# Half of the columns in the recurrence levels of a three-layer kernel

## The reference, cut to what matters

```python
def rwkv7_scan(r, w, k, v, kk, a):
    decay = jnp.exp(-jnp.exp(w))
    b = kk * a
    def step(S, inp):
        r_t, d_t, k_t, v_t, kk_t, b_t = inp
        sa = jnp.einsum('bhij,bhj->bhi', S, -kk_t)
        S = S * d_t[:, :, None, :] + sa[..., None] * b_t[:, :, None, :] + v_t[..., None] * k_t[:, :, None, :]
        return S, jnp.einsum('bhij,bhj->bhi', S, r_t)
```

## Time and profile before

| | |
|---|---|
| median of 3 runs | 3526.99 us |
| time of the profiled execution | 3526.12 us |
| its span | 3524.0 us |
| TensorE busy | 3456.2 us (98% of the span) |
| VectorE, ScalarE, GpSimd busy | 2423.2, 1642.0, 289.4 us |
| mean granted TensorE clock | 0.995 |
| the six pairs of the recurrence | from about 371 to 692 us |

### The profile page before, as it was taken

The page is one execution under the profiler, slowest core; times in us unless marked ns, Lnnn a source line. Parts: engine busy times, 40 slices in busy tenths (PEclk is TensorE's granted clock), DMA queues, the critical chain, the costliest instruction groups (busy, mean ns, idle before and its releaser), DMA issues.

```text
span 3524.0 us, 75021 instructions
## 1 busy us (share of the span) xinstructions
PE 3456.2 (98%) x27870; PEld 3151.2 (89%) x27870; DVE 2423.2 (69%) x3490; ACT 1642.0 (47%) x2248; POOL 289.4 (8%) x358
## 2 busy tenths in 40 slices
PE   8999999999999999999999999999999999999998
PEld 8999888899988899999888888888899988888886
DVE  6986777755676677976756565677766865656566
ACT  6456334444444434754444444444444644434344
POOL 5000234200020000002000000020000200000002
PEclk9999999999999999999999999999999999999999
DMA  7444222255655555555565555555554555555564
GB/s 253 160 156 144 86 86 86 82 171 179 204 191 188 184 178 175 168 169 181 185 194 181 194 185 193 182 188 191 174 161 162 173 185 185 191 185 194 181 194 140
DMA packets 164985, 604.04 MB, mean 171 GB/s; under 512 B 18336, under 2 KB 18464, under 8 KB 164560
## 3 DMA queue, kind: packets, MB, share of 16 engines
q1 hardware_dynamic: 163584, 596.16, 51.8%
q10 hardware_dynamic: 1040, 3.16, 0.2%
q0 software_dynamic: 192, 2.23, 0.2%
HBM read 599.38 MB, written 2.10 MB: 171 GB/s over the span
## 4 chain that ended last, share of the span: by engine, by line
PE 90%; DVE 6%; ACT 2%; issue 1%; POOL 0%; DMA 0%; ACTq 0%; DVEq 0%; POOLq 0%
PE bank L366 35%; PE bank L369 18%; PE bank L345 11%; PE bank L346 10%; PE bank L347 10%; PE bank L1349 4%; DVE w_lo L334 2%; ACT w_hi L325 1%; POOL x_norm_acc L466 0%; DVE nrm_kk L1039 0%; DVE X L2900 0%; PE bank L848 0%; DVE X L2904 0%; PE bank L731 0%; DVE conv_sq L2584 0%
## 5 line engine op out<-in xcount | busy, mean ns | idle before, releaser
L325 ACT ACTIVATE w_hi<-raw 128x1024 fp32r<-128x1024 f32 x1126 | 1157.6, 1053 | 827.2 <-PE bank L369 510.5
L334 DVE TENSOR_TENSOR w_lo<-raw,w_hi 128x1024 fp32r<-128x1024 f32 x1126 | 1350.0, 1236 | 99.9 <-ACT w_hi L325 99.6
L366 PE MATMUL bank<-hid,w_hi 128*128 128x512 f32 x2048 | 643.4, 395 | 0.0
L366 PE MATMUL bank<-u,w_hi 128*128 128x512 f32 x1536 | 484.4, 397 | 0.0
L345 PE MATMUL bank<-hx,w_hi 128*128 128x256 f32 x1568 | 466.1, 297 | 12.1 <-DVE w_lo L334 12.1
L369 PEld LDWEIGHTS bank<-hid,w_lo 128*128 128x128 f32 x2048 | 384.7, 188 | 90.9
L346 PE MATMUL bank<-hx,w_hi 128*128 128x256 f32 x1568 | 445.3, 284 | 0.0
L347 PE MATMUL bank<-hx,w_lo 128*128 128x256 f32 x1568 | 444.9, 284 | 0.3 <-issue 0.3
L366 PE MATMUL bank<-xh,w_hi 128*128 128x512 f32 x1312 | 413.5, 397 | 2.7 <-DVE w_lo L334 2.7
L369 PE MATMUL bank<-hid,w_lo 128*128 128x256 f32 x2048 | 402.3, 278 | 0.0
L369 PEld LDWEIGHTS bank<-u,w_lo 128*128 128x128 f32 x1536 | 289.5, 189 | 69.2
(11 more groups left out here) (477 smaller groups left out, 5559.3 us busy)
## 6 DMA issues: line engine op xcount, KB each, us to landing
raw<-stream SPq DMA_DIRECT2D x1126, 512.0 KB, 4.0
x_raw<-xT SPq DMA_DIRECT2D x4, 512.0 KB, 7.5
mem_raw<-memT ACTq DMA_DIRECT2D x4, 512.0 KB, 9.5
x_res<-xT POOLq DMA_DIRECT2D x1, 2048.0 KB, 9.7
out<-X SPq DMA_DIRECT2D x3, 512.0 KB, 2.7
cst<-consts SPq DMA_DIRECT2D x1, 1504.0 KB, 13.6
out<-X SPq DMA_DIRECT2D x2, 256.0 KB, 2.2
w_sb<-w ACTq DMA_DIRECT2D x1, 384.0 KB, 4.8
```

Of the source, the lines that this page charges most:

```text
L325: nc.scalar.activation(w_hi[:, slot], raw[:, slot], ACT.Copy).then_inc(hi_ready, 1)
L334: nc.vector.tensor_tensor(w_lo[:, slot], raw[:, slot], w_hi[:, slot].bitcast(F), ALU.subtract).then_inc(lo_ready, 1)
L366: nc.tensor.matmul(bank[:], w_hi[:, slot, i], both(moving, kt), start=kt == 0, stop=False)
```

## The change

Joining two halves changes only part of each matrix. X, and what is added to `tm`, differ from zero only in columns whose token number has bit l equal to d; what is added to `u`, only in columns with bit l equal to 1 - d. The helper `with_bit` takes these 32 of 64 columns as a pattern: runs of 2^l columns, every second run. X, T and U now move 32 columns each. ScalarE copies, and VectorE adds, 128 elements a partition where they did 256. U needs the whole of `x` as its stationary operand, so the other half of `x` must be zero. Each level gets an `x` of its own (level 1 in the old place, levels 2 to 5 in the places of `kat`, `krt`, `kbd`, `bbd`, which are no longer read by then), and GpSimd zeroes the half that is never written (`rest_zero`), ten memsets a pair. ScalarE's wait for U of the level before goes, one for the memset comes, and GpSimd waits for TensorE's `u0_1` before level 2.

```diff
--- before.py
+++ after.py
@@ -979,9 +979,10 @@
             o = B + 82 * K + 20 * K * d
             w = {}
 
-            for k, n in enumerate(("abd", "rbd", "bbd", "kbd", "mt", "tm", "brt", "btok", "ktok", "nkatv", "kat", "krt", "u", "x")):
+            for k, n in enumerate(("abd", "rbd", "bbd", "kbd", "mt", "tm", "brt", "btok", "ktok", "nkatv", "kat", "krt", "u")):
                 w[n] = at(f"{n}{d}", o + K * k, [P, NCH, CH])
 
+            w["x"] = {l: at(f"x{l}_{d}", o + K * k, [P, NCH, CH]) for l, k in enumerate((13, 10, 11, 3, 2), 1)}
             w["ml"] = {l: at(f"ml{l}_{d}", o + 13 * K + K * l, [P, NCH, CH]) for l in range(1, LEVELS)}
 
             for n, k in (("e3", 12), ("th", 13), ("s", 15), ("ad", 17), ("bb", 18), ("kd", 19)):
@@ -1049,8 +1050,9 @@
         ST = range(NCH)
         D2 = range(2)
         rw_o = Steps(sem("rwkv_pool"), ["w2t", "a2t", "vbd"] + [f"{n}{d}" for d in D2 for n in ("kbd", "rbd")]
-                     + [f"{n}{d}" for d in D2 for n in (("t1_", "ml1_", "u0_", "u1_") if d == 0 else ("t1_", "ml1_"))]
-                     + [f"ml2_{d}" for d in D2] + ["u1_1"] + [f"ml{l}_{d}" for l in LV if l > 2 for d in D2])
+                     + [f"{n}{d}" for d in D2 for n in (("t1_", "ml1_", "x1_", "u0_", "u1_") if d == 0 else ("t1_", "ml1_", "x1_"))]
+                     + [f"{n}2_{d}" for d in D2 for n in ("ml", "x")] + ["u1_1"]
+                     + [f"{n}{l}_{d}" for l in LV if l > 2 for d in D2 for n in ("ml", "x")])
         rw_v = Steps(sem("rwkv_dve"), [f"{n}{d}" for d in D2 for n in ("u", "s")] + [f"{n}{d}" for d in D2 for n in ("ad", "bb", "t", "kd")]
                      + [f"{n}{d}" for d in D2 for n in ("abd", "bbd")]
                      + [f"{n}{d}" for n in ("mt", "kat", "m", "brt", "krt") for d in D2] + ["ks", "ksr", "q"]
@@ -1127,6 +1129,12 @@
         def halves():
             return [slice(CH * h, CH * h + CH) for h in range(2)]
 
+        def with_bit(ap, l, bit):
+
+            if len(ap.shape) == 3:
+                ap = ap.rearrange("p c i -> p (c i)")
+            return ap.rearrange("p (g b t) -> p g b t", b=2, t=1 << l)[:, :, bit]
+
         def chunk_of(d, s):
             return s if d == 0 else NCH - 1 - s
 
@@ -1145,11 +1153,15 @@
                     rw_o.done(nc.gpsimd.tensor_tensor(w["kbd"][:], chunks(w["kd"][:]), chunks(w["e3"][:]), ALU.mult), f"kbd{d}")
                     rw_o.done(nc.gpsimd.tensor_tensor(w["rbd"][:], chunks(rkv[:, p]), w["e1"], ALU.mult), f"rbd{d}")
                 ident = four(const("istack"))
+
+                def rest_zero(l, d):
+                    rw_o.done(nc.gpsimd.memset(with_bit(dirs[d]["x"][l][:], l, 1 - d), 0.0), f"x{l}_{d}")
                 for d, w in enumerate(dirs):
 
                     need(pool, rw_v, f"m{d}", p)
                     rw_o.done(nc.gpsimd.tensor_tensor(w["tm"][:], w["tm"][:], ident, ALU.add), f"t1_{d}")
                     rw_o.done(nc.gpsimd.tensor_tensor(w["ml"][1][:], w["mt"][:], level(1), ALU.mult), f"ml1_{d}")
+                    rest_zero(1, d)
                     if d == 0:
                         rw_o.done(nc.gpsimd.tensor_tensor(w["u"][:], w["mt"][:], level(0), ALU.mult), f"u0_{d}")
                         need(pool, rw_o, f"u0_{d}", p)
@@ -1160,7 +1172,9 @@
                             if l == 2 and d == 0:
 
                                 need(pool, rw_v, "q", p)
+                                need(pool, rw_p, "u0_1", p)
                             rw_o.done(nc.gpsimd.tensor_tensor(w["ml"][l][:], w["mt"][:], level(l), ALU.mult), f"ml{l}_{d}")
+                            rest_zero(l, d)
                     if l == 2:
                         u = dirs[1]["u"]
                         need(pool, rw_v, "u0_1", p)
@@ -1205,10 +1219,8 @@
                 for l in LV:
                     for d, w in enumerate(dirs):
                         need(act, rw_p, f"X{l}_{d}", p)
-                        if l > 1:
-
-                            need(act, rw_p, f"U{l - 1}_{d}", p)
-                        rw_a.done(nc.scalar.activation(w["x"][:], value_part(bank_of(d, 1), 0), ACT.Copy), f"X{l}_{d}")
+                        need(act, rw_o, f"x{l}_{d}", p)
+                        rw_a.done(nc.scalar.activation(with_bit(w["x"][l][:], l, d), with_bit(bank_of(d, 1)[:, 0:T], l, d), ACT.Copy), f"X{l}_{d}")
                     if l in TILE_2:
                         split_hi(act, pair_tile(p, 2).later(), (TILE_2.index(l),))
                 for s in ST:
@@ -1289,7 +1301,7 @@
                     for d, w in enumerate(dirs):
                         if l < LEVELS - 1:
                             need(v, rw_p, f"T{l}_{d}", p)
-                            rw_v.done(nc.vector.tensor_tensor(w["tm"][:], w["tm"][:], value_part(bank_of(d, 0), 0), ALU.add), f"T{l}_{d}")
+                            rw_v.done(nc.vector.tensor_tensor(with_bit(w["tm"][:], l, d), with_bit(w["tm"][:], l, d), with_bit(bank_of(d, 0)[:, 0:T], l, d), ALU.add), f"T{l}_{d}")
                         if d == 1 and l == 1:
                             split_lo(v, pair_tile(p, 1).later(), (1,))
                         if d == 1 and l == 3:
@@ -1297,7 +1309,7 @@
                         if d == 1 and l in (2, 4):
                             split_lo(v, pair_tile(p, 2).later(), (l // 2 - 1,))
                         need(v, rw_p, f"U{l}_{d}", p)
-                        rw_v.done(nc.vector.tensor_tensor(w["u"][:], w["u"][:], value_part(bank_of(d, 2), 0), ALU.add), f"U{l}_{d}")
+                        rw_v.done(nc.vector.tensor_tensor(with_bit(w["u"][:], l, 1 - d), with_bit(w["u"][:], l, 1 - d), with_bit(bank_of(d, 2)[:, 0:T], l, 1 - d), ALU.add), f"U{l}_{d}")
                 for s in ST:
                     now, old = s % 2, (s - 1) % 2
                     for d in D2:
@@ -1357,8 +1369,11 @@
                 def both(*products):
 
                     for c in range(NCH):
-                        for bank, o, lhs, rhs, cross, name in products:
-                            last = heads2(bank[:, o + CH * c:o + CH * c + CH], lhs[:, c], rhs if rhs is istack else rhs[:, c], cross=cross)
+                        for bank, o, lhs, rhs, cross, name, *columns in products:
+                            dst, moving = bank[:, o + CH * c:o + CH * c + CH], rhs if rhs is istack else rhs[:, c]
+                            if columns:
+                                dst, moving = with_bit(dst, *columns), with_bit(moving, *columns)
+                            last = heads2(dst, lhs[:, c], moving, cross=cross)
                             if c == NCH - 1:
                                 rw_p.done(last, name)
 
@@ -1418,7 +1433,7 @@
                         need(pe, rw_a, f"ktok{d}", p)
                     else:
                         need(pe, rw_v, f"T{l - 1}_{d}", p)
-                    return bank_of(d, 1), 0, w["ml"][l], w["tm"], d, f"X{l}_{d}"
+                    return bank_of(d, 1), 0, w["ml"][l], w["tm"], d, f"X{l}_{d}", l, d
 
                 def level_known(l, d):
                     need(pe, rw_a, f"X{l}_{d}", p)
@@ -1432,11 +1447,11 @@
 
                 def level_t(l, d):
                     level_known(l, d)
-                    return bank_of(d, 0), 0, dirs[d]["u"], dirs[d]["x"], d, f"T{l}_{d}"
+                    return bank_of(d, 0), 0, dirs[d]["u"], dirs[d]["x"][l], d, f"T{l}_{d}", l, d
 
                 def level_u(l, d):
                     level_known(l, d)
-                    return bank_of(d, 2), 0, dirs[d]["x"], dirs[d]["u"], 0, f"U{l}_{d}"
+                    return bank_of(d, 2), 0, dirs[d]["x"][l], dirs[d]["u"], 0, f"U{l}_{d}", l, 1 - d
 
                 for l in LV:
                     if l == 1:
```

## The result

| | before | after |
|---|---|---|
| median | 3525.48 us (20 runs, 3524.24 to 3530.01) | 3543.41 us (all 20 runs; 3543.04 of the 19 used below) |
| ratio after / before, of the mean times | | 1.0044, interval 1.0031 to 1.0058 |
| profiled execution: time, span | 3526.1, 3524.0 us | 3556.07, 3554.3 us |
| its mean granted TensorE clock | 0.995 | 0.983 |

The change made the kernel slower by 0.44% in the mean (0.5% by the medians), and the forecast of 3524 us was wrong: its range ended at 3530. One of the 20 runs after took 4621.86 us; it is left out of what follows, as are the few such runs of the other kernels. The other 19 spread over 3526.40 to 3563.95 us, some six times the spread of before, and their times go with their mean granted clock: 3526.40 and 3528.2 us at 0.993, 3533.3 at 0.991, 3541.25 at 0.989, 3549.01 at 0.986, 3556.07 at 0.983, 3563.95 at 0.981.

What follows compares the result with a forecast made beforehand. TensorE's own pace, set by weight loads, was taken to bound the pairs. Terms 0 - 1.6 - 0.8 - 0.4 = -2.8 us took the profiled 3526.1 to 3523.3, median 3524.2; forecast 3524 us, own range 3520 to 3528, overall 3512 to 3530.

Steps and rivals of the forecast that it cites:

- Streaming 32 columns: X, T and U in the levels: weight loads set the 55 ns pace, so halving moved columns gains 0.
- a gain of 26: Best bound for streaming: pace halves to 27 ns per quarter, 20 groups in 6 pairs, 26 us.
- dear short runs: Rival: level 1's runs of two columns cost four times the price per column, 12 us slower, 3536 us; chance 0.04.
- the 7% for "slower": Chance 0.07 for a slower kernel: late GpSimd memsets (0.03, 3534 us) and short runs costing more (0.04, 3536 us).
- The pace halves: Rival: the matmul's own streaming makes the 55 ns in the levels, 26 us more gained, 3500 us; chance 0.10.
- a part of it: Rival: a fixed piece of the 55 ns is the matmul's, pace falls by a fifth, -11 us, 3513; chance 0.05.
- The ends of the groups: Last matmul ends 27 ns earlier where TensorE goes from quarters to full array, 10 times a pair: -1.6 us.
- The rule that the prediction set against this term: Trainium skill: below about 60 columns matmul latency no longer falls; then the sum would be -1.1 us, not -2.8.
- ScalarE, VectorE, GpSimd: Shorter copies of `x` -0.8 us, shorter adds -0.4, 60 memsets of 206 ns at cost 0.
- The wait of the last U: At level 5, the 0.27 us wait for ScalarE's copy shrinks by 0.134 us, 6 times: -0.8 us.
- the 0.027 from an earlier end of X: At level 5, X ending 0.027 us earlier adds to the copy's 0.107 in shortening the last U's wait.
- TensorE's waits for `tm`: Waits for VectorE's adds, 0.6 us in all: shorter adds remove most, -0.4 us, bounds 0 and -0.6.

Runs made afterwards that it cites:

- the one-run kernel: Changed kernel with the 32 columns as one run at every level, so the inverse is not computed; 3540.31 us, ratio 1.0044 against the kernel before.
- the loads experiment: Changed kernel plus two groups of 8 products a pair at level 3: 64 weight columns with 16 moved, 32 with 32 moved; 3544.85 us.

## Why the prediction was wrong

- **The failed step is "Streaming 32 columns. By the above, 0."** The pace was rightly read as set by the loads. But the term was closed there: with the pace the same, half of the streaming time became time in which a quarter waits for weights, and I never asked what the clock would do. I had written down the granted clock of 1.00 as a given. The runs put some 4 to 41 us in this term (3526.40 and 3563.95, less 3525.48, plus 2.7), about 8 for each pair whose clock falls; in the median it is 3543.41 - 3525.48 + 2.7 = 20.6 us. Full streaming takes all of it away. Full streaming in U alone does so as well (3523.67 us); with only U halved a part of the loss is left.
- **The bounds of that term were one-sided.** They ran from 0 to a gain of 26. The only loss that I allowed it, dear short runs, was a price per column, and the one-run kernel refutes it. None of my rivals named the clock, so the 7% for "slower" lay on mechanisms that did not happen. That the sign came out on their side is no credit to them.
- **The pace halves, or a part of it:** out. A half level takes 1.60 us, and the loads experiment shows why. (In the single records a quarter starts one matmul every 58.4 ns, not 55, and the starts of the two quarters of U are 7 ns apart and not 27.)
- **The ends of the groups** (-1.6 us) did not come. From the start of U to the dense step behind it is 0.57 us with 32 columns and 0.56 with 64, and the duration of a small matmul is the same 219 ns. The rule that the prediction set against this term is what came out; by the prediction's own terms its sum would be -2.8 + 1.6 + 0.16 = -1.0, not the -1.1 given.
- **ScalarE, VectorE, GpSimd:** the durations were 279, 286 and 205 ns for 278, 284 and 206 forecast. The wait of the last U fell by 0.08 us, not 0.13; with all 64 columns moving it fell by 0.11 (to 0.16), the 0.107 of the copy, so the 0.027 from an earlier end of X did not come. TensorE's waits for `tm` (0.6 us) are gone. No TensorE wait is for a memset; one wait of ScalarE, of 2.0 us, ended with one, and TensorE's waits for ScalarE's `x` fell all the same, from 1.6 to 0.8 us in all. With all columns moving, copies, adds and memsets together gave -2.7 us by the medians for a forecast of -1.2; the interval of the ratio, -4.9 to +1.4 us, holds both.
- **My own first theories** also needed mending: that X and T would count in proportion, and that level 5 alone decides. Neither held.

**What stays open.** Why halving U counts and halving X and T doesn't was only argued: in the single records of a group of U, two quarters start 7 ns apart and then nothing starts for 52 ns, while in the interleaved groups four start within 20 ns and the gap is 38 ns. With half the columns a pause in which no quarter streams is therefore longest in U. No run varied this gap by itself. Why the same kernel has a fall in some pairs and executions and not in others is not shown, beyond the gaps that stand ahead of the falls; nor where these gaps come from. No run shows a version without any fall that streams 32 columns in all three products.

## What to carry to other kernels

Where a weight load sets the pace, as the 58.4 ns of a quarter here, moving fewer columns doesn't make TensorE faster, and it can make it slower: ask of each edit that thins TensorE's work what becomes of the granted clock, above all where the work behind it is sparse. "Busy 98%" doesn't answer this; compare the granted clock by stretch, and the number of matmuls in it. When runs of one kernel suddenly spread, set time against mean clock run by run before any other theory. And to speed up small tiles, cut the columns of the weights, not the moving ones: that took a quarter from 58.4 to 31.7 ns, though the kernel that did it in the last U alone gained only 1.8 us, within the noise.

## What the runs showed of the hardware that I had not expected

- The granted clock halves with only short idle gaps in the records ahead of it: 1.39, 0.58 and 0.19 us in the first pair, and 1.10, 0.58 and 0.16 at the same places in the kernel that streams 64 columns and keeps 1.00 there. In the stretch at 0.50 TensorE is busy for 23.00 of 23.00 us. Once low, it stayed so for 20 to 24 us of sparse state products, and with twice the dense work among them for 13.7.
- The recorded duration of a dense matmul understates what half the clock costs: L346 goes from 0.28 to 0.41 us, but in a dense run, as in these rows at 1.00, one matmul follows another every 0.12 us, and at 0.50 every 0.21 (432.92 to 433.13 above).

```profile
437.41 0.28 PE L345 MATMUL bank<-hx,w_hi 128*128 128x256 f32 x1
437.53 0.28 PE L346 MATMUL bank<-hx,w_hi 128*128 128x256 f32 x1
437.65 0.28 PE L347 MATMUL bank<-hx,w_lo 128*128 128x256 f32 x1
```

- The state stage takes 20.40 us for 12.70, 1.6 times as long, and so less than the 1.8 times of the dense pace: part of it is not paced by TensorE's matmuls. Which part, no run shows.
- The recorded duration of a small matmul does not tell its cost: 219 ns at 64 and at 32 moving columns, 206 at 16, 192 with 32 columns of weights, while the pace of a quarter is 58.4, 58.4, 58.4 and 31.7 ns.
- Starts in different quarters can be 7 ns apart. Of matmuls back to back the Trainium skill, "TensorE: Matmul & The Clock Gate", section "Wait — 56ns, not 53.3ns?", says that their starts are never closer than about 25 ns, however few columns move. In these records one quarter by itself keeps to that (31.7 ns at the closest pace), the array with several quarters at work does not.
